# HGRN, MLA, mLSTM and retention mixer: where the modulation weights ride in a ring of three slots

## The reference, cut to what matters

```python
mod = silu(c) @ w_mod[l] + b_mod[l]          # 6 x 1024 values; the same with c_ctx for the context rows
sh1, sc1, g1, sh2, sc2, g2 = split(mod, 6)
o = mixer(rms_norm(x, norm1_g) * (1 + sc1) + sh1)   # MLA attention, HGRN2, mLSTM, retention, each through w_in,
                                                    # then sum over n of sigmoid(gate n) * (branch n @ w_branch[n]), @ w_out
x = x + g1 * o
x = x + g2 * (square(relu((rms_norm(x, norm2_g) * (1 + sc2) + sh2) @ w_ff1)) @ w_ff2)
```

## Time and profile before

| | |
|---|---|
| median of 3 runs | 1738.52 us (1735.85 to 1738.62) |
| the profiled execution, its own time | 1738.21 us |
| its span, first to last instruction | 1736.3 us |
| TensorE matmul busy | 1609.8 us, 93% of the span |
| VectorE, ScalarE, GpSimd busy | 815.1, 744.6, 202.9 us |
| granted TensorE clock, mean | 0.963 |

### The profile page before, as it was taken

How to read it: one execution, slowest core, us unless ns; L and a number is a source line. 1 busy time by engine, 2 the same in 40 slices (tenths; PEclk the granted TensorE clock), 3 DMA queues, 4 the chain that set the end, 5 groups by cost and what they waited for, 6 DMA issues and landing times. The chain is left out here.

```text
span 1736.3 us, 23499 instructions
## 1 busy us (share of the span) xinstructions
PE 1609.8 (93%) x9818; PEld 1302.1 (75%) x9818; DVE 815.1 (47%) x1269; ACT 744.6 (43%) x1065; POOL 202.9 (12%) x172
## 2 busy tenths in 40 slices
PE   5986999999989999889999999888899889989998
PEld 3775786775657768667777777678788667989998
DVE  4376425554453225532223322549447564565553
ACT  5654224344626423433113321464345757455352
POOL 0000001231201110022002200000002401203030
PEclk8998999998999999899999999988899999989999
DMA  8331233221212143244434434231232224436552
GB/s 343 113 130 50 75 128 115 95 75 61 88 52 91 56 158 109 85 170 170 161 134 166 164 135 162 73 122 42 91 143 71 97 76 146 137 143 219 174 191 97
DMA packets 36441, 213.00 MB, mean 123 GB/s; under 512 B 3888, under 2 KB 7344, under 8 KB 12656
## 3 DMA queue, kind: packets, MB, share of 16 engines
q1 hardware_dynamic: 36336, 211.50, 33.9%
HBM read 209.39 MB, written 2.10 MB: 122 GB/s over the span
## 5 line engine op out<-in xcount | busy, mean ns | idle before, releaser
L535 PE MATMUL ps<-parts,whi 128*128 128x512 f32 (+1 forms) x928 | 336.7, 363 | 11.3 <-DVE SQ L1997 6.4
L537 PE MATMUL ps<-parts 128*128 128x512 f32 (+1 forms) x960 | 333.6, 348 | 0.0
L1029 PE MATMUL ps<-parts 128*128 128x512 f32 (+1 forms) x960 | 323.1, 337 | 0.0
L536 PE MATMUL ps<-parts,whi 128*128 128x512 f32 (+1 forms) x928 | 322.7, 348 | 0.0
L1027 PE MATMUL ps<-parts 128*128 128x512 f32 (+1 forms) x928 | 314.9, 339 | 0.0
L1028 PE MATMUL ps<-parts 128*128 128x512 f32 (+1 forms) x928 | 312.6, 337 | 0.0
L1746 DVE TENSOR_TENSOR parts<-ring,parts 128x1024 fp32r<-128x1024 f32 x124 | 147.6, 1231 | 249.0 <-ACT parts L1326 249.0
L1326 ACT ACTIVATE parts<-ring 128x1024 fp32r<-128x1024 f32 x124 | 124.4, 1050 | 263.9 <-PE ps L1029 251.8
L1720 DVE TENSOR_TENSOR parts<-ring,whi 128x1024 fp32r<-128x1024 f32 (+1 forms) x136 | 164.9, 1254 | 135.2 <-ACT whi L1274 135.0
L535 PEld LDWEIGHTS ps<-parts,whi 128*128 128x128 f32 x928 | 179.0, 193 | 50.2 <-issue 27.7
L537 PEld LDWEIGHTS ps<-parts 128*128 128x128 f32 x960 | 184.5, 192 | 23.6
(11 more groups left out here) (271 smaller groups left out, 2177.5 us busy)
## 6 DMA issues: line engine op xcount, KB each, us to landing
ring<-in_w_ff SPq DMA_DIRECT2D x64, 1024.0 KB, 4.8
ring<-in_w_in SPq DMA_DIRECT2D x60, 1024.0 KB, 5.0
ring<-in_w_mod SPq DMA_DIRECT2D x40, 1024.0 KB, 4.8
arena<-in_w_mod SPq DMA_DIRECT2D x8, 1024.0 KB, 20.2
ring<-in_w_branch SPq DMA_DIRECT2D x32, 256.0 KB, 5.4
ring<-in_w_out SPq DMA_DIRECT2D x8, 1024.0 KB, 4.9
arena<-in_tables_rt SPq DMA_DIRECT2D x2, 1280.0 KB, 8.4
X<-in_x SPq DMA_DIRECT2D x2, 1024.0 KB, 6.6
```

The lines of the kernel that those rows point to most:

```text
L535: pe.matmul(ps[0:m, 0:n], w_hi[:, k, c], x_hi[:, k, 0:n], start=(k == 0), stop=False)
L536: pe.matmul(ps[0:m, 0:n], w_hi[:, k, c], x_lo[:, k, 0:n], start=False, stop=False)
L537: last = pe.matmul(ps[0:m, 0:n], w_lo[:, k, c], x_hi[:, k, 0:n], start=False, stop=(k == KD - 1))
L1029: last = pe.matmul(ps[:, 0:nt], w_lo[:, k, c], x_hi[:, k, 0:nt], start=False, stop=(k == kt - 1))
```

## The change

Four modulation blocks of layer 0 leave the ladder. Behind the projections stand now only four (blocks 8 to 11, behind hq, hv, rq, rk), not eight. HGRN's gate blocks carry 12 to 15 (they carried 16 to 19), MLA's 16 to 19 (they carried 20 to 23). Blocks 20 to 23 go behind the first four steps of layer 0's feed-forward, and layer 1's 24 blocks behind six of every seven of the steps after that (they stood behind three of every four of all steps). The first pack of eight is split in two of four, so there are seven packs, not six, and the packs in the feed-forward are closed at steps 4, 13 and 22, not at 10 and 21. The 64 KB of `mg` lose their slot in both layers: they are loaded into columns 2048 and on of `mo`'s slot, which has 2560. `mo`'s slot is given free by the gate product.

The order of the ring from `hg` on in layer 0, after: hg, mq, mk, mv, mo with mg, rq, mod 10, rk, mod 11, rv, rg.

```diff
@@ extra()
     if stage == "ff":
-        return [("mod", 1, i - i // 4)] if i % 4 != 3 else []
+        j = i - 4 - (i - 4) // 7
+        return [("mod", 0, 20 + i)] if i < 4 else [("mod", 1, j)] if (i - 4) % 7 != 6 else []
     if stage == "in":
         return [("mod", 0, 8 + IN_EXTRA.index(i))] if i in IN_EXTRA else []
     n, j = i
-    return [("mod", 0, {HG: 16, MLA: 20}[n] + j)] if n in (HG, MLA) else []
-
-
-IN_EXTRA = ("hq", "hv", "hg", "mq", "mk", "mv", "rq", "rk")
-
-PACKS = [(0, 8, 8), (0, 16, 4), (0, 20, 4), (1, 0, 8), (1, 8, 8), (1, 16, 8)]
+    return [("mod", 0, {HG: 12, MLA: 16}[n] + j)] if n in (HG, MLA) else []
+
+
+IN_EXTRA = ("hq", "hv", "rq", "rk")
+
+PACKS = [(0, 8, 4), (0, 12, 4), (0, 16, 4), (0, 20, 4), (1, 0, 8), (1, 8, 8), (1, 16, 8)]
...
-FF_PACKS = {10: PACKS[3], 21: PACKS[4]}
+FF_PACKS = {4: PACKS[3], 13: PACKS[4], 22: PACKS[5]}
@@ weight_plan()
-        for n in ("hff", "hfb", "hq", "hv", "hg", "mq", "mk", "mv", "mo", "mg", "rq", "rk", "rv", "rg"):
+        for n in ("hff", "hfb", "hq", "hv", "hg", "mq", "mk", "mv", "mo", "rq", "rk", "rv", "rg"):
@@ sources()
                 a, b = IN_COLS[key[2]]
-                return [(0, KD * (b - a), io["w_in"][l, :, KD * a:KD * b])]
+                last = [(2048, 2048 + KD * 16, io["w_in"][l, :, KD * b:KD * (b + 16)])] if key[2] == "mo" else []
+                return [(0, KD * (b - a), io["w_in"][l, :, KD * a:KD * b])] + last
@@ gate_products(l)
-                new_last[("in", l, "mg")] = ("mgp", l)
+                new_last[("in", l, "mo")] = ("mgp", l)
@@ gate_high(l); gate_low(l) likewise
-                raw = weights(act, ("in", l, "mg"))[:, 0:KD * 16].rearrange("p (k c) -> p k c", k=KD)
+                raw = weights(act, ("in", l, "mo"))[:, 2048:2048 + KD * 16].rearrange("p (k c) -> p k c", k=KD)
```

More of the change, by code:

```diff
@@ L1069, in _ @@
                 if l:
-                    modulation_columns(PACKS[5])
+                    modulation_columns(PACKS[6])
                 fill([("hv", j) for j in range(4)])
@@ L1582, in _ @@
                 if l:
-                    modulation_rows(PACKS[5])
+                    modulation_rows(PACKS[6])
                 for name in ("hff", "hfb", "hq"):
@@ L1722, in gate_low @@
             def gate_low(l):
-                i = place[("in", l, "mg")]
-                a = (i % SLOTS) * SLOT
+                a = (place[("in", l, "mo")] % SLOTS) * SLOT + 2048
                 raw = ring[:, a:a + KD * 16].rearrange("p (k c) -> p k c", k=KD)
@@ L2225, in _ @@
                 if l:
-                    modulation(PACKS[5])
+                    modulation(PACKS[6])
                 part_low(l, ("in", "hg"))
```

## The result

The changed kernel takes 1735.85 us in the median of 20 executions (1738.57 before). The ratio to the kernel before is 0.9935, with a 95% interval of 0.9908 to 0.9962: faster by 0.65%, so 1726.9 where the profiled execution of before had 1738.21. One of the 20 executions, with 2667.62 us at a mean granted clock of 0.553, and one of the kernel before, with 1870.27 us, stand apart and are left out of the ratios and of all that follows. The kernel before has two groups too, near 1738.5 and 1753.3 us (69 and 48 of 117 executions over all comparisons). That is why the median of all moved by 2.7 us only while each group moved by 12 and 17. What separates the groups in the changed kernel is shown under the experiments.

The account below looks back on a forecast made before the run. TensorE was taken as the bound except in layer 0's ladder, where engines wait for one another. 1738.21 - 15.4 (ladder) + 4.8 (feed-forward blocks) + 0.35 (pack) = 1728.0 us, range 1722.5 to 1734.5.

Parts of the forecast that it names:

- The ladder, 15.4 us: Layer 0's ladder: with mv and mo loaded a projection earlier, all after it moves up by 7.68 + 7.75 us.
- Both waits: VectorE's waits for the masks of levels 8 and 32 in layer 0's ladder, 7.68 and 7.75 us, go whole.
- The cost that I had bounded by 0 to 0.5: Ladder: slow level 2 makes mq's last product 1.2 us later, the level 8 mask 0.4 us behind VectorE.
- The 256 step: End of layer 0's ladder, 5.32 us, partly at half clock: possible gain counted as 0, bounded by 1.5 us.
- the 4 that I had named as a sign: Sign in the profile after: TensorE's busy time from 83.5 to the gate product is lower by 4 us.
- The blocks in the feed-forward, 5.15 us: Layer 0's feed-forward: four more blocks at 1.19 us each cost 4.8 us, one more pack 0.35 us.
- mg's slot, 0 to 1 us: mg in mo's slot: layer 1 gains 0, bounded by 0 to 1 us, with rq a block nearer.
- The sum, 1728.0: Whole kernel: the profiled 1738.21 us less 15.4, plus 4.8 and 0.35, held to be valid for a median too.
- the stated range: Whole kernel: the time lies from 1722.5 to 1734.5 us.
- The rival for "more": Ladder: no clock fall to 0.50, levels 8 and 32 faster, plus 256 step and layer 1: 1723.1 us; chance 0.14.
- The stall at 752: Early feed-forward of layer 0: TensorE waits 4.79 us for a modulation load at 752.37, the same before and after.

Follow-up runs that it names:

- late loads: The changed kernel with layer 0's mv load held until mq's last product and mo's until mk's, no work added; ratio 0.9987.
- dummy products: The changed kernel with four groups of float32 products, as long as modulation blocks, put back into layer 0's ladder without their loads; ratio 0.9921.
- the two kernels without the stall: The changed kernel without blocks 20 to 23 in layer 0's feed-forward (stage 387.5 us), and with no block behind step 1 (392.8 us, ratio 0.989).
- the moved tile: The changed kernel with one merge tile moved between mLSTM value products and the next head's scores, heads 1 to 3, both layers; 1749.6 us, ratio 1.0044.
- the kernel without the tail: The changed kernel without blocks 20 to 23 of layer 0 and their pack, result not the reference's; 1712.5 to 1729.7 us in 6 executions.
- Dense products in one place: The changed kernel with six dense products between mLSTM value products and the next head's scores, heads 1 to 3 of layer 0; ratio 0.9935.
- dense products in two places: The changed kernel with no block behind step 1, one behind hg, and four dense products before and four behind layer 0's mLSTM value products; ratio 0.9903.

## Why the prediction was right, point by point

**The ladder, 15.4 us.** The gate product moved by 16.6, and by 17.0 from the ladder's own start, which lies 0.45 later in this profile (83.96 and 83.51). Both waits went as worked out: scaling for level 8 starts 7.17 us earlier, that for level 32 15.0, and with the 0.45 this is 7.6 and 15.45 (7.68 and 15.43 expected). The cost that I had bounded by 0 to 0.5 and counted as 0 was 0, with nothing to spare: the gap before level 2 grew to 3.33 us, level 2 ran partly at half clock, and `mq`'s last product came at 124.8 and not 123.5. But the mask of level 8 ended at 129.36, and VectorE was ready at 129.30. The 256 step gave 1.6 (3.72 us against 5.32), which I had bounded by 1.5 and counted as 0; what ran at half clock before did not in this profile. That is the 1.2 us by which the move of 16.6 exceeds 15.4, with the later start. TensorE's busy time up to the gate product fell by 6.4 us (94.95 to 88.58), not by the 4 that I had named as a sign. That the mechanism is the loads, not TensorE's time, is shown from both sides (late loads, dummy products).

**The blocks in the feed-forward, 5.15 us.** By difference of the two kernels without the stall 5.3; between the first and the last block of the stage 367.3 - 362.4 = 4.9. The stage as a whole was 3.9 longer in the first profile, as its start, which runs on a recovering clock, was 1.0 shorter.

**mg's slot, 0 to 1 us.** In layer 1 `rq`'s load is early now, and the rest of the program did not get shorter (630.1 before, 631.0 to 633.3 in the kernels with the change's blocks or `mg`'s slot, the moved tile and the kernel without the tail apart). The zero holds for layer 0's ladder; in layer 1 a gain below 1 us would be lost among differences in clock.

**The sum, 1728.0.** The ratio makes 1726.9 of the profiled execution, the first group has its median at 1726.7. The profiled one has 1736.04, and the median of all 20, 1735.85, lies above the stated range: of this the prediction said nothing. It read the mLSTM stage in one profile, where the clock stood at 1.00, and took this for the property of the kernel. About four of ten executions of both kernels lie in the second group. In the changed kernel's profiles of it the clock is lost in the mLSTM stage; for the kernel before that is not shown. The rival for "more" looked for the clock in the ladder only. That the ratio came out right in spite of this gap is luck: both kernels have a second group about equally often (48 of 117 and 14 of 31), 14.8 us behind the first before and 9.7 after. Within a group the sum is right by its terms.

**The stall at 752.** I took it as it was, 4.8 us, the same before and after. It was the same, but its real price is 6.5 us, as the clock falls during it, and it was to be had by leaving one place empty. For the kernel's reader this was worth more than the tail cost.

## What to carry to other kernels

A ring of few slots is a schedule: a small block between two large ones delays the load two places on, so read which wait a load's issue stands behind before moving compute. Where an engine's queue mixes preparation for later with work that others wait for now, a late load in the first stalls the second. Blocks are free where the engine waits anyway (before level 2, before the norm), and dear behind a slot that is freed late. And take several executions before reading a gain of 1% from a median: two groups can hide it. A mark is best counted from the start of its own stage: 1.5 us that seemed to be `mg`'s stood there before the ladder began.

## What the runs showed of the hardware

TensorE's granted clock fell to 0.50 (1.2 GHz) while its row was busy for the whole time: after 1.13 us of products of 4 rows and two to three us of products with 65 columns, in some profiles and not in others with the same instructions, at a price of 6.4 us for each long fall and 3.3 for the short one at the stage's start. Dense products in one place of each such stretch came with a fall half as long, dense products in two places with none of the long ones in the one profile taken. The Trainium skill ("TensorE: Matmul & The Clock Gate", "A second HAM failure mode: psum-queue depth-cycling") tells of a clock that swings in a kernel which is idle for very short times between groups of matmuls; here no row shows such idle times in the stretch, as far as modelled ends can tell. Why one execution falls and the next doesn't stays open. The profiles show that light work precedes the falls. The narrower spreads, of 12 and 6 executions, speak for dense work between it making the times steadier.
